# Sparse attention in a decoder trunk: waits per PSUM bank, the order of VectorE's small steps, and three steps for GpSimd

## What is computed

```python
def block(args):                       # 128 queries at a time, 4 blocks
    blk, cq_b, w_b = args
    q_pos = blk * Q_BLOCK + jnp.arange(Q_BLOCK)
    q_idx = (cq_b @ w_qidx).reshape(B, Q_BLOCK, HI, DI)
    dots = jnp.einsum('bthd,bsd->btsh', q_idx, k_idx) * (DI ** -0.5)
    score = jnp.einsum('btsh,bth->bts', jax.nn.relu(dots), w_b)
    score = jnp.where(causal[None], score, -jnp.inf)
    _, sel = lax.top_k(score, top_k)                 # 128 keys of each query
    c_sel = c_kv[batch_ix, sel]
    q = (cq_b @ w_uq).reshape(B, Q_BLOCK, H, dh)     # 8 heads of 128
    q_lat = jnp.einsum('bthd,rhd->bthr', q, w_uk)
    logits = jnp.einsum('bthr,btkr->bthk', q_lat, c_sel) * (dh ** -0.5)
    p = jax.nn.softmax(logits, axis=-1)
    o_lat = jnp.einsum('bthk,btkr->bthr', p, c_sel)
    return jnp.einsum('bthr,rhd->bthd', o_lat, w_uv)
```

## Time and profile before

| | us |
|---|---|
| median of 3 runs | 1966.27 |
| lowest, highest | 1966.14, 1966.46 |
| the profiled execution, whole | 1965.35 |
| its span, first to last instruction | 1963.5 |
| matmuls busy in it | 1942.2 |
| projections' last products to the end of the last step, about | 75 |

### The profile page before, as it was taken

The page is one execution under the profiler, slowest core; times in us unless marked ns, Lnnn a source line. Parts: engine busy times, 40 slices in busy tenths (PEclk is TensorE's granted clock), DMA queues, the critical chain, the costliest instruction groups (busy, mean ns, idle before and its releaser), DMA issues.

```text
span 1963.5 us, 23704 instructions
## 1 busy us (share of the span) xinstructions
PE 1942.2 (99%) x9192; PEld 1617.2 (82%) x9192; DVE 1465.2 (75%) x1858; ACT 892.3 (45%) x1244; POOL 219.8 (11%) x163
## 2 busy tenths in 40 slices
PE   9999999999999999999999999999999999999998
PEld 7888888888888888888888888888897898888886
DVE  8999944886767859999833999983369769989722
ACT  6555632352434435555621555562168445554510
POOL 0000012000000031000021000002145440000121
PEclk9999999999999999999999999999999999999999
DMA  5243132331313320422232242223222014222331
GB/s 173 86 144 114 59 103 92 127 134 43 135 42 134 128 87 15 154 90 86 89 103 87 102 155 87 86 89 103 87 94 75 1 59 157 86 86 101 104 101 61
DMA packets 76189, 189.53 MB, mean 97 GB/s; under 512 B 4144, under 2 KB 12336, under 8 KB 73008
## 3 DMA queue, kind: packets, MB, share of 16 engines
q1 hardware_dynamic: 76080, 188.04, 27.5%
HBM read 185.92 MB, written 2.10 MB: 96 GB/s over the span
## 4 chain that ended last, share of the span: by engine, by line
PE 88%; DVE 8%; issue 2%; ACT 1%; SPq 0%; DMA 0%; POOL 0%; DVEq 0%; ACTq 0%
PE bank L2454 12%; PE bank L2456 12%; PE bank L2455 12%; PE bank L2446 12%; PE bank L2448 12%; PE bank L2447 12%; PE bank L2675 3%; PE bank L2673 3%; PE bank L2674 3%; PE bank L2554 2%; DVE part_lo L1563 1%; DVE idx_scores L2255 1%; DVE best L2251 1%; PE bank L2684 1%; PE bank L2930 1%
## 5 line engine op out<-in xcount | busy, mean ns | idle before, releaser
L1022 ACT ACTIVATE part_hi<-quad_w 128x1024 fp32r<-128x1024 f32 x280 | 293.4, 1064 | 277.6 <-PE bank L2456 193.5
L1563 DVE TENSOR_TENSOR part_lo<-quad_w,part_hi 128x1024 fp32r<-128x1024 f32 x280 | 330.1, 1219 | 23.3 <-ACT part_hi L1022 23.0
L2446 PE MATMUL bank<-gated_hi,out_hi 128*128 128x512 f32 x704 | 274.7, 390 | 0.0
L2448 PE MATMUL bank<-gated_hi,out_lo 128*128 128x512 f32 x704 | 274.0, 389 | 0.0
L2447 PE MATMUL bank<-gated_lo,out_hi 128*128 128x512 f32 x704 | 273.9, 389 | 0.0
L2454 PE MATMUL bank<-part_hi,s_hi 128*128 128x512 f32 x640 | 252.3, 394 | 1.2 <-DVE part_lo L1563 1.2
L2456 PE MATMUL bank<-part_hi,s_lo 128*128 128x512 f32 x640 | 249.4, 390 | 0.0
L2455 PE MATMUL bank<-part_lo,s_hi 128*128 128x512 f32 x640 | 249.2, 389 | 0.0
L2454 PE MATMUL bank<-part_hi,xn_hi 128*128 128x512 f32 x608 | 237.3, 390 | 1.6 <-DVE part_lo L1563 1.6
L2455 PE MATMUL bank<-part_lo,xn_hi 128*128 128x512 f32 x608 | 236.6, 389 | 0.0
L2456 PE MATMUL bank<-part_hi,xn_lo 128*128 128x512 f32 x608 | 236.6, 389 | 0.0
(11 more groups left out here) (306 smaller groups left out, 3536.9 us busy)
## 6 DMA issues: line engine op xcount, KB each, us to landing
quad_w<-w_ffn_in SPq DMA_DIRECT2D x80, 1024.0 KB, 7.3
out_raw<-w_ffn_out SPq DMA_DIRECT2D x64, 704.0 KB, 4.2
quad_w<-w_ret_in SPq DMA_DIRECT2D x14, 1024.0 KB, 7.3
rest_raw<-w_ffn_in SPq DMA_DIRECT2D x32, 256.0 KB, 5.5
quad_w<-w_ret_in SPq DMA_DIRECT2D x16, 512.0 KB, 5.2
quad_w<-w_ret_out SPq DMA_DIRECT2D x8, 1024.0 KB, 5.3
w_raw<-w_dsa SPq DMA_DIRECT2D x7, 1024.0 KB, 4.9
x_res<-x_in SPq DMA_DIRECT2D x8, 256.0 KB, 6.3
```

The lines of the kernel that those rows point to most:

```text
L1022: nc.scalar.activation(in_four(part_hi[part_slot(h)]), source, copy).then_inc(part_hi_made, 1)
L1563: nc.vector.tensor_tensor(in_four(part_lo[part_slot(h)]), source, in_four(part_hi[part_slot(h)]).bitcast(FP32), ALU.subtract)\
L2446: mm(to, w_hi_of[:, at:at + width], hi, start=start, stop=False)
L2448: return mm(to, w_lo_of[:, at:at + width], hi, start=False, stop=stop)
```

## The change

Six edits, all in the sparse attention. (1) TensorE no longer waits for all 24 copies ahead of step 0: the transposes of step 1 wait for the copy of tile 20 (bank 4), the results of step 0 for that of tile 21 (bank 5), the results of step 4 for all 24. (2) ScalarE splits the second output unit behind copy 16 instead of copy 19, and makes a four-column Exp behind copy 17, ahead of which the Exp table is loaded. (3) One of the four rounds of the last block ahead of step 0 moves: its `find_8` to step 16 behind `invert(16)`, its `mark_8` to step 17 behind the reciprocal. (4) In steps 6, 10 and 14 VectorE makes the low part ahead of `minimum(i + 2)`, not behind it. (5) In the same three steps GpSimd makes the normalising multiply. (6) The low part number 6, so far in step 30 behind `invert(30)`, now stands in step 31 behind `invert(31)`.

```diff
-    POOL_STEPS = range(2 * HEADS, 3 * HEADS)
-    ROUNDS_AT = {17: 2, 18: 2, 19: 2, 20: 2, 21: 2, 22: 2}
+    LOW_PART_STEPS = [6, 10, 14]
+    POOL_STEPS = LOW_PART_STEPS + list(range(2 * HEADS, 3 * HEADS))
+    FIRST_ROUND = 16
+    ROUNDS_AT = {FIRST_ROUND: 1, 17: 2, 18: 2, 19: 2, 20: 2, 21: 2, 22: 2}
     EARLY_ROUNDS = TOP_K // 8 - sum(ROUNDS_AT.values())
...
-                    elif j in (14, 19):
-                        split_unit(u0 + 8 + j // 19)
+                    elif j in (14, 16):
+                        split_unit(u0 + 8 + j // 16)
+                    if j == 17:
+                        nc.scalar.activation(head_r_col[:, :], minus_half[:, :4], ACT.Exp)
                     if j in FIRST_EXPS:
                         exps(FIRST_EXPS.index(j))
...
+                    if i == FIRST_ROUND:
+                        find_8(last_block)
+                    if i in LOW_PART_STEPS:
+                        result_lo(RESULT_AT.index(i - 1))
                     if i + 2 < len(STEPS):
                         minimum(i + 2)
-                    if i - 1 in RESULT_AT:
+                    if i - 1 in RESULT_AT and i not in LOW_PART_STEPS and i + 2 < len(STEPS):
                         result_lo(RESULT_AT.index(i - 1))
-                    for n in range(ROUNDS_AT[i] if i in ROUNDS_AT and i != CHOICE_STEP else 0):
+                    if i == len(STEPS) - 1:
+                        result_lo(len(STEPS) // 4 - 2)
+                    for n in range(ROUNDS_AT[i] if i in ROUNDS_AT and i not in (FIRST_ROUND, CHOICE_STEP) else 0):
...
                     else:
-                        pe.wait_ge(probs_done, i + 1 - (len(POOL_STEPS) if i in range(3 * HEADS, 4 * HEADS) else 0))
+                        pe.wait_ge(probs_done, i + 1 - len([e for e in POOL_STEPS if e < i]))
                     if i >= 2:
                         pe.wait_ge(probs_t_copied, i - 1)
+                    if i == 1:
+                        pe.wait_ge(proj_copied, PROJ_BANKS.index(4, 20) + 1)
...
                 def results(i):
                     b, h = STEPS[i]
                     pe.wait_ge(probs_t_copied, i + 1)
+                    if i == 0:
+                        pe.wait_ge(proj_copied, PROJ_BANKS.index(5, 20) + 1)
+                    if i == 4:
+                        pe.wait_ge(proj_copied, 3 * 8)
...
-                pe.wait_ge(proj_copied, 3 * 8)
                 def out_products(to, d, tokens, ks):
```

## The result

| us | before | changed |
|---|---|---|
| median, number of runs | 1965.71, 22 | 1969.12, 22 |
| lowest, highest | 1965.02, 1966.54 | 1963.28, 1971.86 |
| the profiled execution, whole | 1965.35 | 1964.58 |
| its span | 1963.5 | 1962.8 |

The ratio of the times is 1.0014, with 1.0008 to 1.002 as its interval: the changed kernel is some 3 us slower, where 1.3 us faster was forecast, and outside of the range that was given. The ratio is still within 0.2%.

A forecast was written before the change was run, and what follows sets the result against it. TensorE, busy 1942.2 of 1963.5 us, was taken as the bound, with some 5.5 us idle in the attention to win. Start -1.4, low parts +1.2, end -1.1 gave -1.3: 1966.27 to 1964.95 us, range 1963.3 to 1966.2.

The forecast's parts named there:

- the start's term: First transpose of step 0: moved round, waits per bank, earlier split and table together give -1.4 us, bounds -1.5 and -0.7.
- A round later: VectorE ahead of step 0: moving one early round gives -1.52 us, and costs nothing in idle time before later minima.
- Waits per bank, split and table sooner: ScalarE's copies ahead of steps 0 and 1 no longer hold back the round's gain, except 0.1 us for hand-over.
- The 1.62 us of idle time ahead of step 0: TensorE, free at 1506.61, transposes step 0 only at 1508.23, on VectorE's multiply, because VectorE is still in the early rounds.
- The low part ahead of the minimum: Steps 6, 10, 14: the minimum now delays the next step's reciprocal, costing 0.35 + 0.35 + 0.48 = +1.18 us, bounds 0 and 1.18.
- Rival 1: Minima behind the low parts cost nothing, as TensorE has slack between steps 7 and 17: -2.5, 1963.8 us; chance 0.23.
- GpSimd's multiplies at no cost: Steps 6, 10, 14: GpSimd takes some 0.5 and 0.9 us each, off the way of transposes 7, 11, 15; cost 0.
- Rival 3: GpSimd's small multiplies dominated by a fixed cost or semaphores: at 2.4 us each, +1.2 in all, 1967.5 us; chance 0.05.
- The end: Step 31: reciprocal no longer behind low part 6, transpose at 1577.65 to 1577.7 instead of 1578.79, -1.1 us, bounds -0.97 and -1.14.
- The rest of the chain: From first output product to last step: the product starts only some 0.2 us sooner, the last step 1.3 us sooner.
- rival 4: First transpose waits for VectorE even now, or output products wait for the moved round: +0.2, 1966.5 us; chance 0.07.

The follow-up runs named there:

- e1_again: The changed kernel with no edit, eleven more executions and a profile of its own: median 1969.12 us, ratio 1.0012.
- e2_start: The kernel before with only the edits at the start (waits per bank, split and table sooner, one round later): 1968.58 us, ratio 1.0006.
- f3_splitonly: The kernel before with only the split of the second output unit moved behind copy 16: 1972.58 us, ratio 1.0029.
- f4_wait_nolow: The changed kernel with GpSimd's second subtraction waiting for two biases, and the low parts of steps 6, 10, 14 behind the minimum again: 1962.80 us, ratio 0.9984.
- g3_wait_nobank: The changed kernel with GpSimd's second subtraction waiting for two biases, and one wait for all 24 copies ahead of step 0 again: 1964.34 us, ratio 0.9994.
- f1_nosplit: The changed kernel with the split of the second output unit back behind copy 19: 1965.76 us, ratio 0.9999.
- e4_end: The kernel before with only low part 6 moved behind step 31's multiply: 1964.82 us, ratio 0.9992.
- e3_steps: The kernel before with only the low parts ahead of the minima in steps 6, 10, 14 and GpSimd's three multiplies: 1967.16 us, ratio 1.0005.
- g1_wait_nolow_nopool: The changed kernel with GpSimd's second subtraction waiting for two biases, low parts behind the minima and the three multiplies on VectorE again: 1962.67 us, ratio 0.9986.
- f2_bias_wait: The changed kernel with GpSimd's second subtraction waiting until two biases are made: 1963.61 us, ratio 0.9986.

## Why the prediction was wrong

The step that failed is the start's term, -1.4: it took VectorE's `choice_to_bias` as unaffected by where GpSimd's second subtraction stands. In the long executions the start doesn't gain 1.4 us but loses 2.8 at step 0. The other terms of the sum held.

- **A round later, -1.52 and free where it goes: right.** Step 0 is transposed 1.67 us sooner in the short execution (13.43 to 11.76), step 2 1.43 (15.00 to 13.57). The moved `find_8` stands in VectorE's idle time between the minima of steps 17 and 18, and the output products aren't delayed by it.
- **Waits per bank, split and table sooner: this step failed.** ScalarE's work came out as it was worked out: no copy holds step 0 or 1. But the split was costed on ScalarE alone. Its high part releases a subtraction on GpSimd, and that had no line in the sum. The prediction also took VectorE's durations as fixed: `choice_to_bias` isn't in it at all, since it wasn't moved. Its 0.36 became 4.8 in every profile of a long execution (e1_again, e2_start, f3_splitonly), and 19 of 22 are long. The loss is 2.8 at step 0 (13.43 to 16.25) and with the clock 4.2 at the first output product (35.03 to 39.27 in e2_start, which has no other order of the low parts). Without the lock the term is right: in f4_wait_nolow that product comes 1.47 sooner than before. Waiting per bank was worth 0.7 at step 0 (g3_wait_nobank), as the prediction had it, and 0.5 at the output products.
- **The 1.62 us of idle time ahead of step 0 were read as the early rounds' alone.** f1_nosplit shows a second limit close behind: before the change, too, the second subtraction runs until 1503.42 + 4.58 = 1508.00, and a multiply that comes sooner waits for it. The old multiply's row has a trace of it: 0.32 us where the same shape takes 0.29 unheld, ending at 1508.08, which is 0.08 behind the subtraction. In e4_end and e3_steps, with the same start, it takes 0.36 and 0.33 and also ends 0.08 behind. The rounds hid the rest.
- **The low part ahead of the minimum, +1.18: right.** 1.18 in the traces (34.74 against 33.56), 0.8 in the times. From ScalarE's high part (1512.16) to the transpose of step 7 (1514.26) it is 2.10 us; 2.0 was written, and 1.66 stood in the earlier trace rows. Rival 1 falls with it.
- **GpSimd's multiplies at no cost: right.** 0.62 us for 128 columns and 0.93 for 256, where 0.5 and 0.9 were written; without them the first output product comes at the same time (g1_wait_nolow_nopool). Rival 3 falls.
- **The end, -1.1: right.** 1.10 in e4_end's trace, -1.3 in its times, and no idle time ahead of the transpose of step 31.
- **The rest of the chain.** In the short execution the first output product is 0.29 sooner than before (0.2 written) and step 31 1.39 (1.3 written). The sum describes that execution well, and the profile of f2_bias_wait too, all of whose executions are short: from the first product of the projections to the end of the span it is 468.70 us before, 467.33 in the short execution, 467.36 in f2_bias_wait. But of the kernel that was forecast only 3 executions in 22 are so.
- **The rivals** that came out slower were GpSimd's multiplies (rival 3) and a round still on the path (rival 4). What came is no wait for a semaphore, and it strikes an instruction that the change doesn't touch; the rivals had only waits and the moved work. The range took in no bound for it.
- **Small slips of the sums.** By its own terms the forecast is 1966.27 - 1.3 = 1964.97 and not 1964.95, the upper end of the range about 1966.1, and rival 3 turns into a loss at 2.1 us. Nothing hangs on them.

In its median f2_bias_wait is 2.5 us below the kernel before, not the 1.3 of the traces. What is left over, 1.2, would fit e4_end's reading: the old start now and then pays for a clock dip which a start without idle time doesn't have, and the profiled execution of the kernel before, 1965.35, is one without. The spreads point the same way: the 30 runs of the kernel before beside it spread from 1964.77 to 1968.28, the eleven of f2_bias_wait from 1963.29 to 1964.55. But a dip in the first 20 us, as in the short execution, moves single executions too, and no run takes these apart. So this is argued and not shown. Nor is it shown what moves the 0.04 us that lie between the two kinds of the changed kernel.

## What to carry to other kernels

When a transfer of work to an earlier place releases something on GpSimd, lay that GpSimd instruction over VectorE's list and ask what VectorE does meanwhile: a `tensor_scalar` from SBUF to SBUF that meets it can last as long as GpSimd's instruction. Where such a pair can't be kept apart by its place, a semaphore that holds GpSimd back is cheap (0.6 us of GpSimd's time here, 5.5 us won), and another form of the instruction, here one with an operand in PSUM, is a second way. And where one profile is all there is, compare its own time with the median before reading it: here the profiled execution of the changed kernel was 4.5 us below the median, and its trace holds no sign of the fault but a 9.63 in place of a 9.41.

## What the runs showed of the hardware

- VectorE's `tensor_scalar` (SBUF to SBUF, 32 bits) and GpSimd's subtraction exclude each other: 128x384 took 4.80 to 4.83 us instead of 0.36 in three profiles, 128x128 1.86 instead of 0.29. VectorE's `MAX8` and `MATCH_REPLACE8`, and a `scalar_tensor_tensor` with one input in PSUM, ran at their own length beside the same subtraction.
- Where two instructions stand back to back on GpSimd, a VectorE `tensor_scalar` that asks about when the first ends is in a race with the second: at 4.77 us behind the first one's start VectorE came first (one profile), at 4.80 and 4.81 GpSimd did (three).
- TensorE's granted clock fell to 0.50, the level of 1.2 GHz, inside 4.44 us of idle time in e1_again and stayed there until some 5 us behind its end, and in one profile (e4_end) fell to 0.50 behind 1.6 us of it, where two others of the same start (before, e3_steps) stayed at 1.00.
- The load of the Exp table took 1.28 us directly between a copy and the Exp, at its early place too (1499.99 to 1501.29 in the changed kernel, behind a copy that ended at 1499.97). The Trainium skill ("ScalarE: Activation LUTs", What ACT_TABLE_LOAD costs) adds a drain of about 1.38 us; neither kernel's trace shows one.
